# A layer's attention steps: the 256-column query unit projected four steps sooner

## The reference, cut to what matters

```python
h = rms_norm(x, attn_norm)
(mq, mk, mv, nsq, kc, vc, ksl, vsl, kwn, vwn, ngate, mgate) = split(h @ w_in)
y_a = moba_attention(...)      # 8 heads, block of 256, key/value of its own
y_b = nsa_attention(...)       # 8 heads in 2 groups: compressed, selected, window branch
x = x + (sigmoid(g_a) * (y_a @ w_br_moba) + sigmoid(g_b) * (y_b @ w_br_nsa)) @ w_o
x = x + (gelu(conv_a) * conv_b) @ w_down         # conv of rms_norm(x) @ w_up
x = x + sigmoid(x @ w_ple_gate) * (p @ w_ple)
```

## Time and profile before

| what | value |
|---|---|
| median of 3 runs | 957.08 us (955.17 to 957.62) |
| the profiled execution: its own time, its span | 955.18 us, 953.4 us |
| mean granted TensorE clock | 0.976 |
| TensorE matmul busy | 901.3 us, 95% of the span |
| VectorE, ScalarE, GpSimd busy | 436.1, 408.0, 403.3 us |
| chain that ended last | PE 80%, DVE 11%, ACT 4%, issue 3%, DMA 1% |

### The profile page before, as it was taken

How to read it: one execution, slowest core, us unless ns; L and a number is a source line. 1 busy time by engine, 2 the same in 40 slices (tenths; PEclk the granted TensorE clock), 3 DMA queues, 4 the chain that set the end, 5 groups by cost and what they waited for, 6 DMA issues and landing times.

```text
span 953.4 us, 13152 instructions
## 1 busy us (share of the span) xinstructions
PE 901.3 (95%) x4585; PEld 775.5 (81%) x4585; DVE 436.1 (46%) x969; ACT 408.0 (43%) x857; POOL 403.3 (42%) x413
## 2 busy tenths in 40 slices
PE   6998898997989899999999999999999999999998
PEld 6897798896969777778778788888888888888886
DVE  5617657657475665553541654433333442021134
ACT  5222555454454555563343464444444443232231
POOL 4632323324242324365646174554444445454450
PEclk8998999997989989999999999999999999999999
DMA  5755234125012122336653073333333333332314
GB/s 167 161 144 144 50 84 114 41 79 125 20 33 57 45 56 78 125 120 242 208 168 99 22 231 94 96 99 103 106 94 97 100 89 110 92 97 89 99 56 133
DMA packets 101363, 99.31 MB, mean 104 GB/s; under 512 B 15956, under 2 KB 76084, under 8 KB 101300
## 3 DMA queue, kind: packets, MB, share of 16 engines
q1 hardware_dynamic: 101247, 98.48, 35.7%
q10 hardware_dynamic: 53, 0.01, 0.0%
HBM read 87.58 MB, written 10.88 MB: 103 GB/s over the span
## 4 chain that ended last, share of the span: by engine, by line
PE 80%; DVE 11%; ACT 4%; issue 3%; DMA 1%; POOL 0%; SPq 0%; DVEq 0%; ACTq 0%; POOLq 0%
PE banks L1488 24%; PE banks L1490 24%; PE banks L1489 24%; PE banks L1631 2%; PE banks L1542 1%; DVE plain_arena L1238 1%; PE banks L1611 1%; PE banks L1610 1%; DVE plain_arena L1118 1%; ACT split_arena L975 1%; DVE plain_arena L1266 1%; DMA plain_arena<-in_x_dram 1%; PE banks L1568 1%; PE banks L1505 1%; DVE plain_arena L1119 1%
## 5 line engine op out<-in xcount | busy, mean ns | idle before, releaser
L1488 PE MATMUL banks<-split_arena 128*128 128x512 f32 (+4 forms) x1228 | 467.0, 380 | 8.5 <-DVE split_arena L1170 4.7
L1490 PE MATMUL banks<-split_arena 128*128 128x512 f32 (+4 forms) x1228 | 456.7, 372 | 0.0
L1489 PE MATMUL banks<-split_arena 128*128 128x512 f32 (+4 forms) x1228 | 456.7, 372 | 0.0
L692 POOL TENSOR_TENSOR split_arena<-plain_arena,split_arena 128x512 fp32r<-128x512 f32 x184 | 241.1, 1322 | 255.0 <-ACT split_arena L912 235.7
L1488 PEld LDWEIGHTS banks<-split_arena 128*128 128x128 f32 x1228 | 233.2, 190 | 47.1 <-DVE split_arena L1170 5.7
L1490 PEld LDWEIGHTS banks<-split_arena 128*128 128x128 f32 x1228 | 233.2, 190 | 35.4
L1489 PEld LDWEIGHTS banks<-split_arena 128*128 128x128 f32 x1228 | 233.6, 190 | 32.2
L912 ACT ACTIVATE split_arena<-plain_arena 128x512 fp32r<-128x512 f32 x184 | 113.1, 628 | 192.7 <-PE banks L1490 184.8
L1446 DVE SCALAR_TENSOR_TENSOR plain_arena<-banks,plain_arena 128x511 f32<-128x511 f32 x44 | 32.7, 743 | 133.2 <-ACT plain_arena L1017 133.2
L871 ACT ACTIVATE plain_arena<-plain_arena 128x128 f32<-128x128 f32 (+1 forms) x96 | 53.6, 559 | 77.3 <-DVE plain_arena L1266 76.9
L707 POOL TENSOR_SCALAR plain_arena<-plain_arena 128x128 f32<-128x128 f32 (+1 forms) x64 | 38.8, 608 | 98.9 <-DVE plain_arena L1283 98.8
(11 more groups left out here) (161 smaller groups left out, 824.2 us busy)
## 6 DMA issues: line engine op xcount, KB each, us to landing
plain_arena<-in_w_up_dram SPq DMA_DIRECT2D x88, 256.0 KB, 3.1
plain_arena<-in_w_down_dram SPq DMA_DIRECT2D x44, 256.0 KB, 2.6
plain_arena<-in_w_in_dram SPq DMA_DIRECT2D x18, 512.0 KB, 4.8
plain_arena<-in_w_in_dram SPq DMA_DIRECT2D x32, 192.0 KB, 3.3
plain_arena<-in_x_dram SPq DMA_DIRECT2D x8, 512.0 KB, 5.2
gates<-plain_arena SPq DMA_DIRECT2D x16, 256.0 KB, 2.3
plain_arena<-skew SPq DMA_DIRECT2D x16, 256.0 KB, 3.9
plain_arena<-gates SPq DMA_DIRECT2D x16, 256.0 KB, 3.6
```

The source lines that it names most:

```text
L692: pool.tensor_tensor(W2l[:, c % RING, :], raw2[:, c % RING, :], W2h[:, c % RING, :].bitcast(F32), ALU.subtract).then_inc(w2_lo, 1)
L1488: nc.tensor.matmul(o, ah, bh, start=first, stop=False)
L1489: nc.tensor.matmul(o, ah, bl, start=False, stop=False)
L1490: return nc.tensor.matmul(o, al, bh, start=False, stop=last)
```

## The change

Unit 6 is projected in steps 28 to 35 and no longer in steps 32 to 39. Its weights are split in steps 25 to 28 and no longer in steps 26 to 29. Because NORM and VEC are reckoned from the end of the projection, NORM of unit 6 goes from step 40 to step 36, and its four vector turns from steps 43 to 46 to steps 39 to 42. The loads of unit 7, issued in the step of unit 6's split, go out one step sooner. Nothing is added or removed: every instruction of before is there once, in another place.

```diff
@@ -118,13 +118,13 @@
         elif w < 6:
             start, counts, row = b0 - 4, (5, 6, 5, 5, 6, 5), 0
         elif w == 6:
-            start, counts, row = b0, (4,) * 8, 0
+            start, counts, row = b0 - 4, (4,) * 8, 0
         else:
             start, counts, row = b0 - 6, (2,) * 16, 0
         for a, count in enumerate(counts):
             PROJ[start + a] = (w, row, row + count)
             row += count
-        split0 = {6: b0 - 6, 7: b0 - 8}.get(w, b0 - 7)
+        split0 = b0 - 8 if w == 7 else b0 - 7
         for a in range(KT // 2):
             SPLIT[split0 + a] = (w, range(2 * a, 2 * a + 2))
         end = start + len(counts)
```

## The result

The changed kernel takes 949.14 us (median of 6 runs, 946.23 to 951.6). The kernel before, run beside it, takes 955.13 us. The ratio over all runs is 0.9922 with a 95% interval of 0.9907 to 0.9937, so 0.78% faster, about 7.5 us; the two medians alone give 6.0 us. The forecast was 952.1 us, 0.52% faster: the right direction, too small a gain.

What follows compares the result with a forecast made beforehand. TensorE was taken as the bound, busy for 901.3 of 953.4 us. Lost time falls from 18.8 to 13.8 us (3.9 + 1.3 + 6.1 + 2.1, plus 0.4), gaining 5.0: median 957.08 to 952.1 us, range 948.8 to 956.6.

Steps and rivals of the forecast that it cites:

- idle, steps 28 to 31: TensorE's idle time left there after the moved blocks fill the waits: 3.9 us, against 6.56 before.
- clock there: Loss at 1.2 GHz after the change: 1.3 us in steps 28 to 31, 2.1 us in steps 36 to 43.
- idle, steps 36 to 43: TensorE's waits for unit 6's normalise and turns after the change: 6.1 us, against 4.6 before; bounds 3 and 9.
- single products that drain: An allowance of 0.4 us added to the sum after, for products that stand singly and drain.
- The wait of step 29: The 3.93 us wait ahead of unit 5's second turn takes in a 1.5 us block and falls to 2.4 us.
- the wait for the normalise: Ahead of unit 6's first turn: a 6.2 us chain with 4.3 us of TensorE cover leaves 1.9 us.
- the rounds from turn to turn: Unit 6's turns, steps 39 to 42: rounds of 5.5, 3.65 and 2.5 us, with turns waiting 4.2 us.
- the rule on turns that it cites: Transpose-mode turns don't count as busy for the clock, making the fall around step 41 certain, at 2.1 us.
- The split in step 25: Unit 6's earlier split delays unit 5's normalise by 0.4 us, bounds 0 and 0.58; first wait 1.2 us.
- The third, the slower one: The clock falls at 224, stays at 1.2 GHz until 238, and falls again at 262: 959.6 us; chance 0.05.
- The second, round trips come back whole: Steps 40 to 42 behave as 28 to 30 did: gain only 1.5 us, 955.6 us; chance 0.26.
- The first, no fall behind the second wait: Clock stays full through steps 39 to 43, idle time near 5: gain 8 us, 949.0 us; chance 0.18.

Runs made afterwards that it cites:

- e3: The changed kernel with NORM and the four turns of unit 6 left in steps 40 and 43 to 46: 949.38 us, ratio to before 0.9934.
- e2: The changed kernel with unit 6's weight split left in steps 26 to 29, as before: 951.65 us, ratio to before 0.9949.
- after_again: A second set of runs of the unaltered changed kernel, with its own profile: 947.28 us, ratio to before 0.9905.
- e7: The changed kernel with unit 6's turns every second step, in steps 39, 41, 43 and 45: 945.58 us, ratio to before 0.9891.
- e8: The changed kernel with turns of units 5, 6 and 7 every second step and gate rows ahead of a turn: 945.33 us, ratio to before 0.9894.
- e9: The changed kernel with unit 6's turns every second step and gate rows ahead of a turn: 947.85 us, ratio to before 0.9916.
- e4: The kernel before with 52 extra products, results overwritten, in the waits of steps 29, 30, 31 and 43: 952.94 us, ratio 0.9968.

## Why the prediction was right in kind and too small

The steps of the ledger, the sum of idle time and half the slow busy time of TensorE, against the changed kernel's profile:

| term | forecast | measured |
|---|---|---|
| before (forecast: steps 28 to 44; measured: 24 to 48) | 18.8 | 18.8 |
| idle, steps 28 to 31 | 3.9 | 0.84 + 2.50 + 0.07 = 3.41 |
| clock there | 1.3 | 1.71 |
| idle, steps 36 to 43 | 6.1 | 4.28 |
| clock there | 2.1 | 1.71 |
| single products that drain | 0.4 | 0 |
| after | 13.8 | 11.1 |
| gain | 5.0 | 7.7 |

**What held.** The cause: 6.56 us of idle time in steps 28 to 31 took the blocks in. The wait of step 29 was forecast at 2.4 us and is 2.50. The clock falls once behind it and returns before step 32. New waits came ahead of unit 6's turns in steps 40 and 41, the largest at 2.65 forecast and 2.58 measured, with a fall of the clock behind it in one profile of two. Step 44 was forecast to start near 271; it starts at 273.20, of which 1.9 us were there ahead of step 24. e3 shows that the filling carries the gain, e2 that the split must come along.

**The step that failed** is the idle time of steps 36 to 43, "6.1 us, against 4.6 before": 4.28 us, so 1.8 of the 2.7 us by which the gain was missed. Two parts were too large. First, the wait for the normalise, 1.9 us forecast, 0.97 measured. I took the chain from `rstd_begin` to the turn at 6.2 us and its cover at 4.3. It took 257.12 - 251.47 = 5.65 us, and the cover was 4.68 us. VectorE's rows of the chain in the changed kernel:

```profile
251.47 0.17 DVE L1128 TENSOR_SCALAR plain_arena<-plain_arena 128x16 f32<-128x16 f32 x1
...
252.73 0.69 DVE L1379 COPY plain_arena<-banks 128x512 f32<-128x512 f32 x1
...
255.69 2.50 DVE L1238 TENSOR_TENSOR plain_arena<-plain_arena 128x512 f32<-128x512 f32 x4
```

I had allowed for a quieter normalise (2.50 and not 3.18 us) but not for the first row: 0.17 us here, 0.82 in the earlier trace rows. Second, the rounds from turn to turn: 5.21, 3.80 and 2.70 us, where I took 5.5, 3.65 and 2.5. Their sum, 11.7, was right. But TensorE's work in them was longer, since it ran at 1.2 GHz from 267.27, and the third turn did not wait at all: waits of 0.73 (0.58 at the turn, the rest just ahead of it), 2.58 and 0 us, 3.3 in place of 4.2. I counted slow work as lost in full and the wait beside it as lost in full too. The prediction also called a fall of the clock there certain by the rule on turns that it cites; in `after_again` the same turns stood behind the same waits and the clock stayed at 2.4 GHz, so the 2.1 us hung on the execution.

**Smaller errors on the same side.** The split in step 25 was priced at 0.4 us, from unit 4's 14.31 against unit 5's 13.73. The changed kernel has 223.55 - 209.81 = 13.74 us. The lower bound was right: a difference between two places of the kernel was put down to the split without a row for it. The 0.4 us for draining products was a guess.

**Rivals.** The third, the slower one, was to be decided by the clock at step 32: it was back at 233.14, ahead of step 32. The second, round trips come back whole, was wrong: step 40 to 41 took 3.80 us and not 5.1. (Its own sum was unclear too: it has the third round at 5.1 and at 3.7 us in one sentence.) The first, no fall behind the second wait, had the size of the gain, 8 us. In the first profile the clock fell in step 41 all the same, and the size came from shorter waits; in the profile of `after_again` it did not fall, so there this rival was right. The idle time from step 36 was 4.3 and 4.6 us, and not near 5.

**The base.** The forecast took 957.08 us as the time before. With six runs its median is 955.13, but in the later sets it is 955.84 to 957.09, so the base was not the error. The ratio is free of it: 0.9948 forecast, 0.9922 and 0.9905 measured.

## What to carry to other kernels

Where one engine is the bound in some steps and idle in others, add up its idle time and half of its busy time at the lower clock over the stretch that an edit touches: the gain of moving work is the change of that sum. It finds what a stretch loses, but it is not the price of each part: work that runs slower beside a wait costs less than it says. A wait names only what came last. Before moving or spreading the operation that waits, look for the next thing out of the same step of the other engines; in e7 and e8 the wait just went to it, and shortening that step's chain (gate 6 a step sooner) is what took 2.0 us of idle time out of e9's stretch.

## What the runs showed of the hardware

A small VectorE instruction took 0.82 us where it takes 0.17: it began while GpSimd worked on gate 7's weights and ended with that. GpSimd's row in the kernel before:

```profile
264.47 1.79 POOL L672 TENSOR_TENSOR split_arena<-plain_arena,split_arena 128x512 fp32r<-128x512 f32 x1 [1.28 <-ACT split_arena L975]
```

It ends at 266.26, and VectorE's instruction, begun at 265.48, at 266.30. The Trainium skill, "SBUF — State Buffer", section "Who interferes with whom", says that the two engines share a port pair as an exclusive lock, and that when VectorE is in a two-port mode, which it says this kind of instruction (`tensor_scalar`) can enter, the second to issue blocks fully until the first is done. The trace agrees, to 0.04 us; whether the instruction was in that mode no row shows.

The clock was worth about half of what the ledger counts for it. Held at 2.4 GHz, the kernel before gained 3.7 us of the 7.67 us that the ledger counts as lost to it, since much of the slow work stood beside waits that grew when it went faster (1.07 and 0.72 us became 1.51 and 1.21 us in e4).

The length of one wait did not decide whether the clock fell. It fell behind waits of 3.93 and 2.84 us before, and of 2.50 and 2.58 us in the changed kernel. But the same 2.58 us passed without a fall in `after_again`, and waits of 2.35 us in e7 and 2.95 us in e9 did too, where the 2.96 us of e8 brought one. These rows don't settle what decides it.
